# Sums of weights: made on VectorE beside the products, or by DMAs in DRAM ahead of them

## The reference

```python
def sq_relu_mlp(h, w_up, w_down):
    return jnp.square(jax.nn.relu(h @ w_up)) @ w_down
```

```python
c_act = jax.nn.silu(c)
mod = (c_act @ ada_w[l] + ada_b[l])[:, None, :]
sh_t, sc_t, g_t, sh_c, sc_c, g_c = jnp.split(mod, 6, axis=-1)
h = rms_norm_2(x, tm_pre_g[l]) * (1.0 + sc_t) + sh_t
y = token_mixer(h, w_in[l], ...)
```

## Time and profile before

| | |
|---|---|
| Median of three executions | 1982.93 us (1982.1 to 1983.48) |
| The profiled execution | 1981.71 us, its span 1980.0 us |
| Busy: TensorE, VectorE, ScalarE, GpSimd | 1961.3, 1341.7, 894.3, 60.4 us |
| Granted TensorE clock, mean | 0.999 of 2.4 GHz |
| DMA | 209.05 MB, 106 GB/s over the span |

### The profile page before, as it was taken

How to read it: one execution, slowest core, us unless ns; L and a number is a source line. 1 busy time by engine, 2 the same in 40 slices (tenths; PEclk the granted TensorE clock), 3 DMA queues, 4 the chain that set the end, 5 groups by cost and what they waited for, 6 DMA issues and landing times.

```text
span 1980.0 us, 29280 instructions
## 1 busy us (share of the span) xinstructions
PE 1961.3 (99%) x10404; PEld 1640.2 (83%) x10404; DVE 1341.7 (68%) x2145; ACT 894.3 (45%) x1417; POOL 60.4 (3%) x114
## 2 busy tenths in 40 slices
PE   9999999999999999999999999999999999999999
PEld 7777789898987887898988788778888888888888
DVE  6555579687777776797787769574444686563545
ACT  4555554445444554544444443474333544432333
POOL 0000000000110110000001100000000000000000
PEclk9999999999999999999999999999999999999999
DMA  4332243323562114523226513211322412223232
GB/s 158 86 85 85 75 148 129 106 79 98 184 205 78 52 49 157 179 69 106 96 99 214 190 46 104 74 64 65 96 96 98 151 43 85 96 95 105 88 99 91
DMA packets 61292, 209.05 MB, mean 106 GB/s; under 512 B 7160, under 2 KB 10232, under 8 KB 61200
## 3 DMA queue, kind: packets, MB, share of 16 engines
q1 hardware_dynamic: 49920, 168.32, 25.8%
q0 software_dynamic: 10560, 37.28, 6.0%
q10 hardware_dynamic: 720, 2.23, 0.3%
HBM read 205.66 MB, written 2.13 MB: 105 GB/s over the span
## 4 chain that ended last, share of the span: by engine, by line
PE 94%; DVE 4%; ACT 1%; DMA 1%; issue 1%; SPq 0%; DVEq 0%; ACTq 0%
PE bank L893 23%; PE bank L895 23%; PE bank L894 23%; PE bank L1216 4%; PE bank L1218 4%; PE bank L1217 4%; PE bank L1016 1%; PE bank L1091 1%; PE bank L1075 1%; PE bank L998 1%; PE bank L1001 1%; PE bank L1043 1%; PE bank L949 1%; PE bank L951 1%; PE bank L950 1%
## 5 line engine op out<-in xcount | busy, mean ns | idle before, releaser
L893 PE MATMUL bank<-b_hi,w_hi 128*128 128x512 f32 x2060 | 813.0, 395 | 6.6 <-DVE w_lo L2764 4.0
L895 PE MATMUL bank<-b_hi,w_lo 128*128 128x512 f32 x2060 | 802.9, 390 | 0.0
L894 PE MATMUL bank<-b_lo,w_hi 128*128 128x512 f32 x2060 | 802.7, 390 | 0.0
L893 PEld LDWEIGHTS bank<-b_hi,w_hi 128*128 128x128 f32 x2060 | 387.2, 188 | 95.9 <-issue 8.2
L895 PEld LDWEIGHTS bank<-b_hi,w_lo 128*128 128x128 f32 x2060 | 387.0, 188 | 81.0
L894 PEld LDWEIGHTS bank<-b_lo,w_hi 128*128 128x128 f32 x2060 | 387.4, 188 | 80.2 <-issue 2.4
L2764 DVE TENSOR_TENSOR w_lo<-w_raw,w_hi 128x1024 fp32r<-128x1024 f32 (+3 forms) x259 | 306.8, 1185 | 210.2 <-ACT w_hi L1810 209.5
L1810 ACT ACTIVATE w_hi<-w_raw 128x1024 fp32r<-128x1024 f32 (+3 forms) x259 | 265.5, 1025 | 263.3 <-PE bank L895 253.6
L3916 DVE SCALAR_TENSOR_TENSOR arena<-bank,vec,arena 128x511 f32<-128x511 f32 x88 | 65.7, 749 | 85.8 <-ACT arena L2658 80.5
L1216 PE MATMUL bank<-parts,w_hi 128*128 128x256 f32 x384 | 108.7, 283 | 3.3 <-DVE x L3113 3.3
L1218 PE MATMUL bank<-parts,w_lo 128*128 128x256 f32 x384 | 107.9, 281 | 0.0
(11 more groups left out here) (398 smaller groups left out, 2537.9 us busy)
## 6 DMA issues: line engine op xcount, KB each, us to landing
w_raw<-in_wstream SPq DMA_DIRECT2D x253, 512.0 KB, 3.5
arena<-in_ada POOLq DMA_DIRECT2D x48, 512.0 KB, 4.3
plain<-in_wseven SPq DMA_DIRECT2D x24, 512.0 KB, 5.0
early<-in_wseven SPq DMA_DIRECT2D x24, 512.0 KB, 6.8
w_raw<-in_wstream SPq DMA_DIRECT2D x12, 384.0 KB, 3.0
arena<-crow POOLq DMA_DIRECT2D x16, 256.0 KB, 4.8
w_raw<-in_wstream SPq DMA_DIRECT2D x10, 256.0 KB, 2.6
x<-in_xT ACTq DMA_DIRECT2D x4, 512.0 KB, 6.6
```

The source lines that it names most:

```text
L893: nc.tensor.matmul(dst, whi, rhs_hi(k), start=(k == 0), stop=False)
L894: nc.tensor.matmul(dst, whi, rhs_lo(k), start=False, stop=False)
L895: last = nc.tensor.matmul(dst, wlo, rhs_hi(k), start=False, stop=(k == n - 1))
```

## The change

There is a DRAM tensor `seven_sums`. POOL fills it in 15 turns (`sum_turn`), each of up to four DMAs, over groups of two units. For one group the first turn copies the four raw pieces there, the next adds raw pieces to two of them, the next adds one sum to a third, the next another to the fourth. A turn does these four steps for four groups at once, and waits until all DMAs of the turns before have landed. Ten turns are issued in and right after fox, one after the first network's conditioning, four between the heads of mla. The loops of POOL there are written out.

SyncE then loads every piece, raw or sum, as a DMA of its own (256 KB, 28 in a chunk, four of seven from `seven_sums`) into a ring of 8 pieces, two per semaphore. It waits for the turns that a network needs before that network's first piece. `two`, `three` and `four` are gone from VectorE.

The 48 conditionings are laid out anew: in `mla_out` 3 and not 6, beginning at the fourth column tile, in ff_b three in the up tiles and three in the products of each Strassen chunk (one buffer, two regions of `plain` and `early`), 6 in its last up tiles, none beside its last down tiles. The wait for the row at the start of `mla_out` goes to the fourth tile. The mixer's first three panels are split one at a time, each after a column tile of ff_b's last down product. The matmuls and their order are the same.

```diff
@@ program
-        seven_in_to = [b[:, 2:6, :].rearrange("p a t -> p (a t)") for b in (plain, early)]
-        seven_pair = plain[:, 6:8, :].rearrange("p a t -> p (a t)")
+        SEVEN_RING = 8
+        GROUP = 2
...
+        PIECE = (0, None, None, 3, None, None, 2)
+        SUM_AT = (None, 1, 2, None, 0, 3, None)
...
+        def seven_raw(i):
+            r = i % SEVEN_RING
+            return (plain if r < SEVEN_RING // 2 else early)[:, 2 + r % (SEVEN_RING // 2), :]
...
+        SUM_GROUPS = {"ff_a": UNITS // SUM_STEP, "ff_b": 2 * UNITS // SUM_STEP}
+        SUM_TURNS = SUM_GROUPS["ff_b"] + 3
@@ SyncE
-                for h in range(2):
-                    cols = slice(2 * T * h, 2 * T * (h + 1))
-                    sp.dma_start(seven_in_to[n % 2][:, cols], seven_src(n)[:, cols]).then_inc(seven_in[n % 2], 16)
+                if i >= SEVEN_RING and i % GROUP == 0:
+                    sp.wait_ge(seven_lo, seven_count(i - SEVEN_RING + GROUP - 1))
+                n, o = i // SEVEN, i % SEVEN
+                src, at = (seven_rows, PIECE[o]) if PIECE[o] is not None else (sum_rows, SUM_AT[o])
+                sp.dma_start(seven_raw(i), src[n * P:(n + 1) * P, at * T:(at + 1) * T]).then_inc(seven_in[i // GROUP % N_GROUPS], 16)
...
                         sp.wait_ge(free, count)
+                        sp.wait_ge(sum_in, sum_count(SUM_GROUPS[run] + 3))
@@ GpSimd
+            def sum_turn(turn):
+                pool.wait_ge(sum_in, sum_count(turn))
+                for back, (to, src, at) in enumerate(((slice(0, 4 * T), seven_rows, slice(0, 4 * T)),
+                                                      (slice(0, 2 * T), seven_rows, slice(T, 3 * T)),
+                                                      (slice(2 * T, 3 * T), sum_rows, slice(0, T)),
+                                                      (slice(3 * T, 4 * T), sum_rows, slice(2 * T, 3 * T)))):
+                    if 0 <= turn - back < SUM_GROUPS["ff_b"]:
+                        units = slice((turn - back) * SUM_STEP * P, (turn - back + 1) * SUM_STEP * P)
+                        if back:
+                            pool.dma_start(sum_rows[units, to], src[units, at], accum_op=ALU.add).then_inc(sum_in, 16)
+                        else:
+                            pool.dma_start(sum_rows[units, to], src[units, at]).then_inc(sum_in, 16)
...
+            for h in range(MLA_HEADS):
+                m = h % 2
+                pool.wait_ge(rope_hi, h + 3)
+                pool.tensor_tensor(qr_part[1][m], q_rope[m], qr_part[0][m].bitcast(F32), ALU.subtract).then_inc(rope_lo, 1)
+                if m == 0:
+                    sum_turn(FOX_PAIRS + 3 + h // 2)
@@ VectorE
+            def chunk_condition(c, i):
+                if i % SEVEN == 4 and i >= SEVEN:
+                    k = ADA_MORE + 2 * ADA_CHUNK * c + ADA_CHUNK + i // SEVEN - 1
+                    conditioning(k, k % 2, 2)
...
-                        if i % SEVEN == 0:
-                            four(at // SEVEN)
-                        if i % SEVEN == 2 and i + 5 < end:
-                            two(at // SEVEN + 1)
-                        if i % SEVEN == 4 and i + 3 < end:
-                            three(at // SEVEN + 1)
+                        if run == "ff_b":
+                            chunk_condition(c, i)
...
+                last_add(0, 0)
+                for k in range(2, KT):
+                    w_split(last + 1 + k)
+                    last_add(k - 1, (k - 1) % 2)
+                    last_post(k - 2, k % 2)
+                    if k % 2 == 0:
+                        mix_low(k // 2 - 1)
...
-                    lambda: low_context(MLA_HEADS - 1, 0, CTX0["mla"] + MLA_HEADS), lambda: dve.wait_ge(ada_cin, 48), fresh=4)
+                    lambda: low_context(MLA_HEADS - 1, 0, CTX0["mla"] + MLA_HEADS), nothing, fresh=4)
```

More of the change, by code:

```diff
@@ L683, in program, with sum_count @@
         wflat = d["wstream"]
-        def seven_src(n):
-            size = 4 * P * T
-            return d["wseven"][n * size:(n + 1) * size].rearrange("(p c) -> p c", p=P)
+        seven_rows = d["wseven"].rearrange("(r c) -> r c", c=4 * T)
+        sum_rows = nc.dram_tensor("seven_sums", (2 * UNITS * P, 4 * T), F32, kind="Internal").ap()
+        def sum_count(turn):
+            return 16 + 16 * sum(min(max(turn - back, 0), SUM_GROUPS["ff_b"]) for back in range(4))
         block = ctx.enter_context(nc.Block())
@@ L2150, in seven_ffn @@
                 j = first + n - 1
-                def last_square(j):
-                    square(j)
-                    if run == "ff_b":
-                        for p in range(MIX_W):
-                            mix_split(p)
-                segment(run, first + n, KT, last_mid, nothing, lambda: last_square(j), fresh=1)
+                if run == "ff_a":
+                    segment(run, first + n, KT, last_mid, nothing, lambda: square(j), fresh=1)
+                    return last_mid
+                square(j)
+                w_split(first + n + 1)
+                for k in range(2, KT):
+                    w_split(first + n + k)
+                    last_mid(k - 2, k % 2)
+                    if k % 2 == 0:
+                        mix_split(k // 2 - 1)
+                last_mid(KT - 2, 0)
                 return last_mid
@@ L3166, in up_tiles @@
                         else:
-                            n0 = QUAD * seven_chunk(run, c)
-                            two(n0)
-                            low(SEVEN * n0)
-                            low(SEVEN * n0 + 1)
-                            three(n0)
+                            low(SEVEN * QUAD * seven_chunk(run, c))
+                            low(SEVEN * QUAD * seven_chunk(run, c) + 1)
                         if not last:
@@ L3246, in lead1 @@
                         dve.sem_inc(x_sum, 2)
-                        mix_splits()
-                segment(run, last + 1, KT, last_add, last_post, lead0, lead1)
+                if run == "ff_a":
+                    segment(run, last + 1, KT, last_add, last_post, lead0, lead1)
+                    return last_add, last_post
+                w_split(last + 1)
+                lead0()
+                w_split(last + 2)
+                lead1()
+                last_add(0, 0)
+                for k in range(2, KT):
+                    w_split(last + 1 + k)
+                    last_add(k - 1, (k - 1) % 2)
+                    last_post(k - 2, k % 2)
+                    if k % 2 == 0:
+                        mix_low(k // 2 - 1)
                 return last_add, last_post
```

149 lines of the change are left out of this document (76 added, 73 removed).

## The result

| | before | after |
|---|---|---|
| time, median of the runs | 1982.7 us (1982.1 to 1983.48, 4 runs) | 2006.62 us (2004.49 to 2008.41, 4 runs) |
| span of the profiled execution | 1980.0 us | 2006.5 us |
| TensorE busy / VectorE busy | 1961.3 / 1341.7 us | 1968.5 / 1294.4 us |
| GpSimd's DMA queue | 37.28 MB, 6.0% | 88.13 MB, 18.0% |

The ratio is 1.012, with a 95% interval of 1.0102 to 1.0138. The forecast of 1973.7 us was wrong in sign, and the range (to 1986) did not hold the time.

What follows compares the result with a forecast made beforehand. TensorE, busy 1961.3 of 1980.0 us, was taken as the bound, leaving 18.7 us idle. Gains of 9.7 us less 0.5 for late loads made 9.2, so 1982.93 became 1973.7 us, range 1970.5 to 1986.

Steps and rivals of the forecast that it cites:

- The gains: TensorE's waits removed: four for additions to x 3.3 us, mla_out's start 1.8, ff_b's end 4.6; sum 9.7 us.
- the last term: At ff_b's end, splitting mixer panels one by one removes a 2.88 us gap and 1.7 us of clock fall: 4.6 us.
- The conditionings in ff_b's chunks: One 1.22 us conditioning per unit replaces some 2.5 us of sums on VectorE; cost nothing, at most 1 us if late.
- The price of a turn: On the DMA engines, added bytes cost as copied ones: 13.4 us of engines, 22.0 us a full turn.
- deadline of 24.8 us: Before ff_a, turn 9 must land by about 274 us for the silu row and first conditioning loads: 24.8 us a turn.
- first rival: Turns too slow: adding DMAs move bytes twice, 31.6 us a turn, ff_a's first conditioning late, 2018 us; chance 0.20.
- upper bound: Dearest price of a turn: crowded-stretch rate of 148 GB/s with every added byte counted twice, 42 us.
- The row's write: Silu row written on POOL's queue behind turn 9, before ff_a's first conditioning; some 2 us allowed.
- sum for a late turn: Before ff_a, each us a turn takes past 24.8 costs seven times, less TensorE's cover of about one panel, 5.4 us.
- Loads beside turns: Panel loads beside a turn double from 3.5 to 7.0 us, still in time; 0.5 us allowed, bounds 0 and 6.
- late panel loads: Rival: loads beside a turn take 12 to 13 us, three turns stop TensorE, 3 to 6 us, 1977 to 1980; chance 0.12.
- The ring of pieces: In the chunks, two pieces take 5.0 us, issued 7.3 us ahead: hidden; rival of a late ring 1998 us, chance 0.04.

Runs made afterwards that it cites:

- e1: Changed kernel with no turns issued; the summed pieces are read from the weights' own rows instead (wrong numbers); 1972.50 us.
- e8: Kernel before with only the mixer's three early panel splits done one by one between the tiles of ff_b's last product; 1977.89 us.
- e9: Changed kernel, second-network turns moved into ff_a's chunks and beside mla's heads, groups of 2 then 1 units, one turn per fox pair; 1972.83 us.
- e2: Changed kernel with a turn's three adding transfers made plain copies of the same bytes to the same places (wrong numbers); 1985.71 us.
- e4: Changed kernel with only turn 9 moved, behind the loads of the first six conditioning tiles instead of ahead of the silu row's write; 1994.43 us.
- e7: Changed kernel, turn 9's work behind the first conditioning tiles, half-size turns, second-network turns moved into ff_a's chunks and beside mla's heads 1 to 7; 1979.78 us.
- e3: Changed kernel with a turn's 2 MB copy given its two column halves as outer dimension, rows of 4 KB; 2344.90 us.
- e5: Changed kernel with a turn's 2 MB copy issued as two transfers of half the columns, rows of 4 KB; 2020.08 us.

## Why the prediction was wrong

- **The gains: right in sum.** 3.3 + 1.8 + 4.6 = 9.7 us was the sum; e1 measures 9.7, e8 gives 4.3 for the last term, and e9 lies 5.1 us below e8, where 3.3 + 1.8 were forecast for the rest. These two weren't taken apart. The agreement to a tenth is in part luck, since e1 has 1.3 us of new waits that the sum doesn't have.
- **The conditionings in ff_b's chunks: slightly wrong.** "Nothing, and at most 1 us" was counted. The load in time was all that was looked at; a conditioning in time still holds VectorE for 1.22 us, and the last one of each chunk delays the split of a half panel (e1): 1.3 us in three waits, with the clock at full level.
- **The price of a turn: this step failed.** "A byte added at the price of a byte copied" made 13.4 us of engines and 22.0 us a turn. With copies the step holds (20.4 us, e2). An added byte takes twice the engine time, so that a turn is 20.0 us of engines and 27.6 us long. By the prediction's own deadline of 24.8 us a turn that is too late, and the first rival's mechanism is what happened. That rival named the engine time of 20.0 us and the half rate behind it, and it got 0.20. It had too long a turn (31.6 us), since it let a turn take only the 0.69 of the engines that others left, and the others' loads were the ones that gave way (10.0 us to land). Two slips changed nothing in the forecast: that rival's sum gives 324 and not 325 us for turn 9, and the 148 GB/s of the upper bound divide three loads by a time that is the median to landing of one.
- **The row's write: late with the turn.** The prediction let turn 6 go out at 174.8 and turn 9 land at 263, before the write is issued, and so allowed "some 2" us for it. Turn 6 went out at 189.06 and turn 9 only at 271.87, and the write took 24 us, since it stood behind turn 9 on GpSimd's queue. Where turn 9 was through (e2) or stood on its other side (e4) it took 1.9. The place of this one turn is worth 12.2 of the 34.1 us. The prediction's own sum for a late turn gives 7 x (27.6 - 24.8) - 5.4 = 14.2 us, so that with the right price it would have said 1988 us.
- **Loads beside turns: this step failed too.** A load was to double to 7.0 us, for 0.5 us in all, since its slack is 11 us. It took 10.0 at the median. Beside fox's middle pairs that cost nothing, but the slack was read there, and the turns at 260, 610 and 675 us (in e4 at 330 us too) stand in other stretches. Even where the price of a turn was as forecast (e2), the time was 12 us above the forecast. What e4 keeps over e1 is 21.9 us. Half turns took back 3.9 of it, and e7's places with e9's sizes 17.7. The rival "late panel loads" had the mechanism, at 3 to 6 us; it counted the waits, and not the clock that falls behind the longer ones (0.83 in the windows of 620 and 680 us).
- **The ring of pieces: right** in e1 and e9, where no wait for a piece stops TensorE. In e4 ScalarE waits for pieces beside the turn at 330 us, 3.2 and 4.6 us, so the ring isn't deep enough beside a whole turn.

What stays open is why an added byte takes twice the engine time, and what in the edit of e3 makes its copy run at the pace of two engines. Smaller turns than halves weren't tried.

## What to carry to other kernels

Work moved to idle DMA engines isn't free: price an unmeasured kind of transfer from both sides, and if the price decides a deadline, let the chance of the dear side follow from that. Place such transfers by stretch, and not by the mean share: here the same bytes cost 34 us or 0.3 us, depending on what stood beside them and behind them on their queue. Ahead of a small transfer that others wait for, no large one belongs on its queue. When a transfer is slow, look at the engines' share while it runs alone, before its packets are blamed.

## What the runs showed of the hardware

- Additions from DRAM to DRAM ran at 154 GB/s of engine time, copies at 327 in the same place (worked out from the shares of e2 and the changed kernel).
- A 4 KB write behind 4 MB of transfers on its queue landed after 24 us, and after 1.9 with none ahead or all of them through.
- The same 2 MB copy, in rows of 4 KB with its two column halves as outer dimension, ran at the share of two of 16 engines (12.5%) and doubled the turn, to 56 us and more (e3). As two transfers in 4 KB rows it added 2.5 us to a turn (e5).
- Loads on another queue took 10.0 us in place of 3.6 beside the turns with 64 KB rows, 9.7 with 4 KB rows (e5), and 11.6 where the turns only copied (e2).
